# A two-block transformer layer stack in float32: B's products two steps later, cleared matmuls before x, u's end and q's begin by token tile

## The reference

```python
h = _rmsnorm(x, ln1_g)
proj = h @ w_in
q, k, v, u = jnp.split(proj, [ATTN_WIDTH, ATTN_WIDTH + KV_WIDTH, ATTN_WIDTH + 2 * KV_WIDTH], axis=-1)
...
y_attn = _sliding_window_attention(q, k, v, attn_sinks, rel_bias)
y_ssm = _s5_mixer(u, ssm_a_re, ssm_a_im, ssm_log_dt, ssm_b_re, ssm_b_im,
                  ssm_c_re, ssm_c_im, ssm_d, w_glu)
mixed = jnp.concatenate([_rmsnorm(y_attn, attn_out_g), _rmsnorm(y_ssm, ssm_out_g)], axis=-1)
x = x + mixed @ w_out
```

## Time and profile before

| | before |
|---|---|
| median of 3 runs | 3215.51 us (3215.14 to 3215.81) |
| the profiled execution | 3214.15 us |
| its span, first to last instruction | 3212.1 us |
| TensorE busy (matmuls) | 3182.7 us, 99% |
| VectorE busy | 1894.2 us, 59% |
| ScalarE busy | 1506.6 us, 47% |
| granted TensorE clock, mean | 0.999 |

### The profile page before, as it was taken

How to read it: one execution, slowest core, us unless ns; L and a number is a source line. 1 busy time by engine, 2 the same in 40 slices (tenths; PEclk the granted TensorE clock), 3 DMA queues, 4 the chain that set the end, 5 groups by cost and what they waited for, 6 DMA issues and landing times.

```text
span 3212.1 us, 40994 instructions
## 1 busy us (share of the span) xinstructions
PE 3182.7 (99%) x16942; PEld 2651.1 (83%) x16942; DVE 1894.2 (59%) x2085; ACT 1506.6 (47%) x1872; POOL 90.7 (3%) x84
## 2 busy tenths in 40 slices
PE   8999999999999999999999999999999999999998
PEld 6778888888888888888888888888888888888887
DVE  7686555455555646565555555665556655555556
ACT  6655544434444544454444444455344544444443
POOL 1230000000000000000000000000000000000000
PEclk9999999999999999999999999999999999999999
DMA  6364555555555555656656566645555566666554
GB/s 216 120 184 156 185 185 195 185 196 185 196 189 191 191 183 184 219 174 186 194 186 186 182 201 187 212 162 171 170 168 186 188 193 187 193 187 193 184 184 157
DMA packets 214341, 593.37 MB, mean 185 GB/s; under 512 B 12507, under 2 KB 17420, under 8 KB 213644
## 3 DMA queue, kind: packets, MB, share of 16 engines
q1 hardware_dynamic: 214156, 590.77, 57.1%
HBM read 588.60 MB, written 2.12 MB: 184 GB/s over the span
## 4 chain that ended last, share of the span: by engine, by line
PE 95%; DVE 2%; ACT 1%; issue 1%; DMA 0%; POOL 0%; SPq 0%; POOLq 0%; DVEq 0%; ACTq 0%
PE PS L2498 71%; PE PS L2553 13%; PE PS L2556 7%; PE PS L2597 1%; DVE LO L1424 1%; PE PS L2605 0%; ACT HI L732 0%; DMA RAW<-in_w_in 0%; PE PS L2622 0%; PE PS L3026 0%; DMA RAW<-in_w_out 0%; PE PS L2707 0%; PE PS L2519 0%; PE PS L2688 0%; POOL ST L2344 0%
## 5 line engine op out<-in xcount | busy, mean ns | idle before, releaser
L1424 DVE TENSOR_TENSOR LO<-RAW,HI 128x1024 fp32r<-128x1024 f32 (+1 forms) x1104 | 1343.3, 1223 | 1111.3 <-ACT HI L732 1103.5
L732 ACT ACTIVATE HI<-RAW 128x1024 fp32r<-128x1024 f32 (+1 forms) x1104 | 1151.4, 1051 | 1193.7 <-PE PS L2498 927.8
L2498 PE MATMUL PS<-HI,KPA 128*128 128x512 f32 x3520 | 986.3, 394 | 4.1 <-ACT HI L732 1.4
L2498 PE MATMUL PS<-HI,KPB 128*128 128x512 f32 x3392 | 921.0, 390 | 0.0
L2498 PEld LDWEIGHTS PS<-HI,KPA 128*128 128x128 f32 x3520 | 651.7, 188 | 145.0 <-issue 4.9
L2498 PEld LDWEIGHTS PS<-HI,KPB 128*128 128x128 f32 x3392 | 632.8, 188 | 129.8
L2553 PE MATMUL PS<-KPA,HI 128*128 128x512 f32 x1792 | 634.6, 399 | 0.0
L2498 PE MATMUL PS<-LO,KPA 128*128 128x512 f32 x1760 | 548.0, 391 | 1.9 <-DVE LO L1424 1.8
L2498 PE MATMUL PS<-LO,KPB 128*128 128x512 f32 x1696 | 522.9, 390 | 0.0
L2556 PE MATMUL PS<-KPA,LO 128*128 128x256 f32 x1792 | 503.3, 281 | 0.0
L2553 PEld LDWEIGHTS PS<-KPA,HI 128*128 128x128 f32 x1792 | 336.7, 188 | 83.4
(11 more groups left out here) (305 smaller groups left out, 1238.4 us busy)
## 6 DMA issues: line engine op xcount, KB each, us to landing
RAW<-in_w_up SPq DMA_DIRECT2D x128, 1024.0 KB, 5.4
RAW<-in_w_down SPq DMA_DIRECT2D x128, 1024.0 KB, 5.6
RAW<-in_w_qkv SPq DMA_DIRECT2D x48, 1024.0 KB, 5.4
RAW<-in_w_ff_gate SPq DMA_DIRECT2D x88, 512.0 KB, 3.6
RAW<-in_w_ff_up SPq DMA_DIRECT2D x88, 512.0 KB, 4.5
RAW<-in_w_ff_down SPq DMA_DIRECT2D x44, 1024.0 KB, 5.6
RAW<-in_w_in_ab SPq DMA_DIRECT2D x40, 1024.0 KB, 4.9
RAW<-in_w_in SPq DMA_DIRECT2D x16, 1024.0 KB, 5.1
```

Source lines behind the costliest of these rows:

```text
L732: e.activation(HI[plan.slot[s]][:, 0:w], RAW[:, d % NRAW, j, 0:w], ACT.Copy).then_inc(S("hi_made"), 1)
L1424: e.tensor_tensor(LO[h][:, 0:w], RAW[:, d % NRAW, j, 0:w], HI[h][:, 0:w].bitcast(F32), ALU.subtract).then_inc(S("lo_made"), 1)
L2498: ins = e.matmul(PS[:, b + j, 0:cw], l, r[h][:, 512 * j:512 * j + cw], start=(i == 0 and part == 0), stop=(last and part == 2))
```

## The change

It has three parts.

1. The products of B on DVE stand two steps later, and with them `expand` and `turned_b` on ACT and `turn_b` on PE.
2. The loads at the start come in another order: x's first 256 columns first, then the identity, the parameters, the first weights, x's next 256 columns, and the rest of x with the weights; B and C behind all of x. POOL clears a tile IDLE (128x512) and TensorE multiplies it three times by itself, as plain float32, into a PSUM bank that nobody reads; x's first transposes stand behind these.
3. "u" is added to `BY_TILE`.

```diff
-BY_TILE = {n: 2 for n in ("ws0", "ws1", "wa0", "qkv0.0", ...
+BY_TILE = {n: 2 for n in ("u", "ws0", "ws1", "wa0", "qkv0.0", ...
...
+    IDLE = nc.alloc_sbuf_tensor_at("IDLE", [128, 512], F32, offset=ph[0])
...
-        load("ident_loaded", ID[:, :], inp["ident"])
-        load("params_loaded", PAR[:, :], inp["params"])
-        for c in range(4):
+        for half in range(2):
+            c0 = 256 * half
+            load(f"x_first{half}", XR[:, :, c0:c0 + 256], inp["x"][:, c0:c0 + 256].rearrange("(t p) c -> p t c", p=128))
+            if half == 0:
+                load("ident_loaded", ID[:, :], inp["ident"])
+                load("params_loaded", PAR[:, :], inp["params"])
+                weights(0)
+        for c in range(1, 4):
             x_part(f"x_loaded{c}", c)
-            if c == 0:
-                weights(0)
-                load("b_loaded", BB[:, 0, :], inp["ssm_b"][0])
-                load("b_loaded", BB[:, 1, :], inp["ssm_b"][1])
-            elif c == 1:
-                weights(1)
-            elif c == 2:
-                weights(2)
-                load("c_loaded", CC[:, 0, :], inp["ssm_c"][0])
-                load("c_loaded", CC[:, 1, :], inp["ssm_c"][1])
+            if c < 3:
+                weights(c)
+        for part in range(2):
+            load("b_loaded", BB[:, part, :], inp["ssm_b"][part])
+        for part in range(2):
+            load("c_loaded", CC[:, part, :], inp["ssm_c"][part])
...
             e.activation(WV[0:16, :], PS[0:16, 4, 0:383], ACT.Copy).then_inc(S("bias_rows_made"), 1)
-            yield
-            yield
+            for _ in range(4):
+                yield
             expand(0)
...
             yield from eigenvalues()
+            for _ in range(2):
+                yield
             q.wait_ge(S("b_loaded"), 32)
...
+        e.memset(IDLE[:, :], 0.0).then_inc(S("cleared"), 1)
+        mark(S("cleared"))
...
             e.matmul(PS[0:16, 4, 0:383], RB, OH, start=True, stop=True).then_inc(S("bias_rows_done"), 1)
-            for _ in range(10):
+            for _ in range(12):
                 yield
...
+        q.wait_ge(S("cleared"), 1)
+        for _ in range(3):
+            e.matmul(PS[:, 7, :], IDLE[:, 0:128], IDLE[:, :], start=True, stop=True)
         pr = prep()
         unit("kv", norm("xT", x_loaded), [pr], ahead=X_DUE)
```

More of the change, by code:

```diff
@@ L300 @@
 O_DUE = (2, 3, 3, 3, 4, 4, 4, 4)
-BY_TILE = {n: 2 for n in ("ws0", "ws1", "wa0", "qkv0.0", "qkv0.1", "qkv0.2", "qkv1.0", "qkv1.1", "qkv1.2", "wo0.0", "wo0.1")}
+BY_TILE = {n: 2 for n in ("u", "ws0", "ws1", "wa0", "qkv0.0", "qkv0.1", "qkv0.2", "qkv1.0", "qkv1.1", "qkv1.2", "wo0.0", "wo0.1")}
 BY_TILE |= {n: 4 for n in ("oab1", "dn2.0.7.1", "wo1.1", "dn2.1.7.1")}
@@ L1145, in x_loaded @@
         def x_loaded(c, t):
-            q.wait_ge(S(f"x_loaded{2 * c}"), 16)
+            if c == 0:
+                q.wait_ge(S("x_first0"), 16)
+                q.wait_ge(S("x_first1"), 16)
+            else:
+                q.wait_ge(S("x_loaded2"), 16)
             q.wait_ge(S(f"x_loaded{2 * c + 1}"), 16)
@@ L2612, in x_loaded @@
             q.wait_ge(S("ident_loaded"), 16)
-            q.wait_ge(S(f"x_loaded{c // 4}"), 16)
+            q.wait_ge(S(f"x_loaded{c // 4}") if c >= 4 else S(f"x_first{c // 2}"), 16)
         def turn_b(n):
```

## The result

| | before | after |
|---|---|---|
| median | 3214.89 us (3213.66 to 3215.98, 20 runs) | 3219.54 us (3217.63 to 3221.69, 20 runs) |
| the profiled execution, its span | 3214.15, 3212.1 | 3219.07, 3217.1 |

The ratio is 1.0015 (95%: 1.0009 to 1.0022). The predicted time was 3216.3 us.

A forecast was written before the change was run, and what follows sets the result against it. TensorE, busy 99% of the span, was taken as the bound, VectorE in kv. -1.1 -2.2 +0.2 +3.55 +0.35 = +0.8 on 3214.15 gave 3214.95, plus 1.36 for the median: 3216.3 us; range 3212.5 to 3220.5 (0.8).

The forecast's parts named there:

- the likeliest case: Whole kernel: all terms hold and the wait ahead of q costs no clock pace; 3216.3 us, chance 0.50.
- the clock's rival: Ahead of q: the clock falls in the new 4.7 us wait, costing 3.2 us more; 3219.5 us, chance 0.27.
- the 6.4 us line: Whole kernel: 0.2% needed to tell a change from none, below 3209.1 or above 3221.9; no change 0.90.
- Between u and q, +3.55: Ahead of q's first matmul: TensorE idles 4.70 us instead of 1.15 for the read of u; loss 3.55.
- The clock: Behind the wait ahead of q: q's matmuls 0.23 us apart, or 0.43 if the clock fell, 3.2 us more.
- LO wait behind it, +0.35: q's second step: its LO split is due at 1.83 us but there at 2.2; loss 0.35 (0 to 0.6).
- kv, -2.2: End of kv: two VectorE ops leave the row ahead of its last split; gain 2.2 us (0 to 4.0).
- Start, -1.1: Start: second weights land 1.3 us earlier, parameters 1.0 later, so VectorE begins the angles earlier; gain 1.1 (0 to 2.1).
- The cleared matmuls, 0: Start: three matmuls end between 4.6 and 8.0 us within TensorE's slack; cost and gain in pace counted as nothing.
- Last step of u, +0.2: End of u: tile 0's last step starts sooner and waits for its LO split; loss 0.2 us (0 to 0.5).
- TensorE's pace as the start's bound: Start and front of kv: cleared matmuls give back 3.2 us, kv gains up to 4.0; 3212.4 us, chance 0.12.
- the end by tile as a cover for the read: Between u and q: the 1.15 us wait goes and the 3.55 loss doesn't come; 3211.0 us, chance 0.05.

The follow-up runs named there:

- e5: Kernel before with B's products, spreads and transposes two steps later on all three engines, nothing else: 3218.10 us, ratio 1.0011.
- e2: Changed kernel with ScalarE's last spread of C (four ops) moved from ahead of u's first read to behind its second: 3216.04 us, ratio 1.0005.
- e3: Changed kernel without u in the list of units that end by token tile: 3218.93 us, ratio 1.0014.
- e1: Changed kernel with five extra float32 matmuls on TensorE filling the wait ahead of q's first matmul: 3217.80 us, ratio 1.0009.
- e9: Kernel before with B's products, spreads and transposes two steps later, plus five extra matmuls in the wait ahead of q: 3216.05 us, ratio 1.0005.
- e8: Kernel before with VectorE's products of B alone two steps later: 3213.72 us, ratio 0.9998.
- e10: Kernel before with VectorE's products alone two steps later and C's second spread behind u's second read: 3213.07 us, ratio 0.9994.
- e6: Kernel before with the new order of loads, cleared tile and three matmuls, nothing else: 3214.75 us, ratio 1.0001.
- e11: Kernel before with the new order of loads and the cleared tile, without its three matmuls: 3214.92 us, ratio 1.0001.
- e12: Kernel before with the cleared tile and its three matmuls, in the old order of loads: 3215.01 us, ratio 1.0002.
- e7: Kernel before with u by token tile, nothing else: 3214.75 us, ratio 1.0001.
- e4: Changed kernel with B's transposes, spreads and reads back at their old steps, only VectorE's products left late: 3215.79 us, ratio 1.0004.

## Why the prediction was right, and what it missed

The time came 3.2 us above the forecast, outside the likeliest case's own range (3214.5 to 3218.5) and inside the whole one (3212.5 to 3220.5), at the 3219.5 that the clock's rival gave. That "no change" was right hung on the 6.4 us line and not on the likeliest case. That the rival's time fits to 0.04 us is luck: the forecast stood on a median of before of 3215.51, which 20 runs put at 3214.89. By differences, +4.65 was measured, +0.8 forecast, and +4.0 would have been the rival's. By the steps:

- **Between u and q, +3.55.** Right in place, size (4.70 of idle) and releaser. e5 shows the products' part makes it, e2 that the spread's four ops are 2.4 of it, e3 that the order by tile neither makes nor hides it (4.71 without).
- **The clock.** This is the step that failed: the likeliest case held that the wait would not cost TensorE its pace. From q's first matmul to its first SEL it is 6.67 us after (95.67 to 102.34), 3.78 before: 2.89 lost, against 3.2 in the rival. The ground that I gave against it, that no wait of before cost its pace, said nothing on a wait four times as long. The Trainium skill (TensorE: Matmul & The Clock Gate, "Why this matters for your kernels") warns of such gaps between bursts; this trace and e5 agree, with half pace behind 4.7 us. Filled with matmuls the same wait does not bring it (e1, e9): that is shown. The whole time gave back only 1.7 and 2.0 of the 2.9; the rest lies partly in the starts of these executions, but how many of the runs had which fall is not known.
- **LO wait behind it, +0.35.** 0.25 at full pace (e1), covered by the half pace in the change itself.
- **kv, -2.2.** 1.96 (30.49 to 28.53), and the same in e3 to e5 and e8 to e10 within 0.06. The idle at kv_sb grew from 0.17 to 0.46, where 0.2 was added.
- **Start, -1.1.** Only -0.37. The mechanism held: VectorE starts on the angles 1.27 us after the split in before and after (12.74, 12.37), and u follows it by 30.5 in all five kernels with the old kv. The landing was mis-sized: the 402 GB/s of the earlier trace rows was not reached ahead of it. The windows of before at 6 to 8 and 8 to 10 us:

```profile
6.00:8.00 2.00, 1.09 (x4) 0.71 (x4) 0.00 (x0) 0.67 (x2) 2.00 (x1) 1.00 1.04 399
8.00:10.00 2.00, 1.00 (x2) 0.49 (x3) 1.73 (x4) 1.21 (x3) 1.84 (x3) 1.00 1.04 370
```

And of after:

```profile
6.00:8.00 2.00, 1.03 (x5) 0.36 (x3) 0.00 (x1) 1.54 (x4) 2.00 (x1) 1.00 0.99 288
8.00:10.00 2.00, 0.97 (x2) 0.58 (x3) 2.00 (x4) 0.94 (x2) 2.00 (x1) 0.92 0.97 321
```

The last column falls by 111 and 49 GB/s with the DMA engines nearly as busy (0.99 and 0.97 for 1.04): 0.32 MB not moved in these 4 us, 0.8 us at 402 GB/s, of the 1.3 counted. It is the new order's doing and no accident of one execution: at 6 to 8 us the seven kernels with it have 240 to 323 GB/s, the seven with the old one 396 to 407. The shorter rows of x's 256-column loads may be why; that wasn't tried. The parameters came 1.63 later (5.32), not 1.0, yet GpSimd had the angles at 11.47, where 11.5 was forecast. Nothing of this front shows in a median (e6, e11): the split stood at 10.69 to 12.55 with the new order and at 11.45 to 12.48 with the old, a spread greater than the gain (means of seven each: 11.43 and 11.90).
- **The cleared matmuls, 0.** Right (e6 with e11, e12). They ended at about 6.5, within 4.6 to 8.0. What I did not see is that TensorE, ahead of its feeders, only waits more: in e1 and e2, 2.77 and 3.71 us for ACT's chunks, with a fall of its clock and 1.1 and 1.6 us lost before u; e12's 2.24 us brought neither.
- **Last step of u, +0.2.** TensorE's LO matmul stands at 85.25 instead of 85.03, where the one ahead of it (84.12 and four of 0.23) would have let it.

In the profiled executions the span grew by 5.0 where the sum had 0.8. The 4.2 between are the clock 2.89, the start 0.73, kv 0.24, the rest of the program 0.55 and 0.14 between u and q, less the LO wait's 0.35. Two rivals fell: TensorE's pace as the start's bound (e12), and the end by tile as a cover for the read (in e7 the wait goes, but LO splits take as much).

## What to carry to other kernels

Work that is moved to relieve one engine must be followed to where its last piece now lands: here 2 us were won at kv's end and 3.55 paid where the moved reads and spreads ended directly ahead of the read that opens q. A wait of TensorE that grows from one to several microseconds has to be priced with the half pace behind it, here 2.9 us on top of 3.55. Moving only the ops that were in the way (VectorE's products), and taking what stood ahead of the read out of its way, gave the lowest median (e10), 1.6 us below before and within the noise.

## What the runs showed of the hardware

- Waits of TensorE of 2.02 (e6), 2.08 (e4), 2.27 (e2), 2.77 (e1), 3.71 (e2) and 4.70 us (after) were each followed by half pace. 2.24 in e12 and 1.93 in e2, both at the start, were not, nor were 1.15 ahead of q (before, e6, e8, e11, e12) and 1.67 in e10's attention. About 2 us the length alone does not say what the clock will do. Two waits of 1.45 and some 0.55 close together, at 8 to 10 us, were followed by half pace in after, e3, e4 and e6 and not in e12, nor were 1.51 and 0.50 in e1.
- The same fall costs differently: behind idles of 4.70 and 4.71, q reached its first SEL in 6.67 (after, e5: 95.83 to 102.50) and 5.38 us (e3: 95.86 to 101.24). That may be part of why the change's runs spread over 4 us and those of before over 2.3.
- The granted-clock column stands at 1.00 in the first 12 us of before though the matmuls run at half pace, and at 0.50 in the same stretch after, with the same 0.43 us from matmul to matmul. At the start the paces are to be read, not the column.
